# A four-sublayer decoder step on eight cores: x tiles loaded ahead of the weights, one ring for all PSUM banks, the next tile's norm ahead of the second group's products, and the program's last block in halves

## The reference

```python
h = x + 0.5 * rmsnorm(swiglu(rmsnorm(x, ffn1_pre_g), gate1, up1, down1), ffn1_post_g)   # FFN 1, 2816 wide
n = rmsnorm(h, mix_pre_g)
b_a, c_a, h_a, u, v = split(n @ w_in)                   # five parts of 512 columns
y_a = b_a * causal_dwconv(conv_prev, c_a * h_a, conv_w) # depthwise, 3 taps
v_n = rmsnorm(v per head of 64, v_norm_g)
y_b = u * (tril(w_s) @ v_n + b_s)                       # per head, over chunks of 128 tokens
h = h + rmsnorm(concat(rmsnorm(y_a, out_g_a), rmsnorm(y_b, out_g_b)) @ w_out, mix_post_g)
h = h + 0.5 * rmsnorm(swiglu(rmsnorm(h, ffn2_pre_g), gate2, up2, down2), ffn2_post_g)
h = h + rmsnorm(sigmoid(h @ ple_w_gate) * (p_emb @ ple_w_proj), ple_post_g)
```

## Time and profile before

| | us |
|---|---|
| median of 3 runs | 1360.84 |
| the profiled execution, whole time | 1360.08 |
| its span on the slowest core (core 2) | 1359.0 |
| shortest span of a core | 1348.5 |
| TensorE busy in that span | 1300.9 |
| VectorE busy | 523.6 |
| ScalarE busy | 410.3 |

### The profile page before, as it was taken

How to read it: one execution, slowest core, us unless ns; L and a number is a source line. 1 busy time by engine, 2 the same in 40 slices (tenths; PEclk the granted TensorE clock), 3 DMA queues, 4 the chain that set the end, 5 groups by cost and what they waited for, 6 DMA issues and landing times.

```text
span 1359.0 us, 18605 instructions; the slowest of 8 cores (1348.5 to 1359.0 us)
## 1 busy us (share of the span) xinstructions
PE 1300.9 (96%) x6770; PEld 650.7 (48%) x6770; DVE 523.6 (39%) x691; ACT 410.3 (30%) x858; POOL 94.3 (7%) x185
## 2 busy tenths in 40 slices
PE   6999999999989999999998999999999799999995
PEld 5566654455535666644433344444444344444442
DVE  3322223357776222213356322124467822212337
ACT  3311112344455111111165211123434611111136
POOL 1100000001001100000001000000010010000000
PEclk8999999999989999999989899999999899999998
DMA  9998322129715963231299983421396297433223
GB/s 214 180 211 181 63 47 47 28 57 164 129 26 103 169 108 63 48 69 26 53 201 232 224 160 67 75 43 31 68 166 116 57 158 143 78 56 62 32 39 124
DMA packets 88185, 139.87 MB, mean 103 GB/s; under 512 B 58272, under 2 KB 58528, under 8 KB 87456
## 3 DMA queue, kind: packets, MB, share of 16 engines
q0 software_dynamic: 25296, 90.25, 40.2%
q1 hardware_dynamic: 62800, 48.43, 13.6%
HBM read 206.03 MB, written 9.51 MB: 159 GB/s over the span
## 4 chain that ended last, share of the span: by engine, by line
PE 84%; DVE 6%; DMA 4%; issue 3%; ACT 2%; DVEq 0%; SPq 0%; ACTq 0%
PE ps L218 55%; PE ps L553 24%; PE ps L542 3%; DVE nT L227 2%; DVE zsc L227 2%; DMA h<-xT 1%; DVE big L231 1%; DMA y<-big 1%; DVE big L227 1%; DMA big<-xT 1%; ACT sg L223 1%; PE ps L498 1%; DVE nbr L227 1%; ACT big L223 1%; ACT L223 0%
## 5 line engine op out<-in xcount | busy, mean ns | idle before, releaser
L218 PE MATMUL ps<-nT,ring 128*128 128x384 bf16 (+1 forms) x4160 | 779.5, 349 | 18.8 <-DVE zsc L227 9.1
L218 PEld LDWEIGHTS ps<-nT,ring 128*128 128x128 bf16 x4160 | 407.9, 98 | 386.3 <-issue 35.4
L231 DVE TENSOR_TENSOR big<-ps,sg 128x384 bf16<-128x384 f32 (+1 forms) x220 | 134.1, 611 | 495.2 <-PE ps L218 476.0
L553 PE MATMUL ps<-ring,big 128*128 128x512 bf16 x1320 | 285.5, 379 | 4.4 <-DVE big L231 4.4
L223 ACT ACTIVATE sg<-ps 128x384 f32<-128x384 f32 (+1 forms) x237 | 126.8, 536 | 508.9 <-PE ps L218 499.9
L553 PEld LDWEIGHTS ps<-ring,big 128*128 128x128 bf16 x1320 | 128.9, 98 | 160.8 <-issue 6.0
L259 POOL DMA_DIRECT2D ring<-w x170 | 89.9, 537 | 1088.4 <-PE ps L218 499.6
L223 ACT ACTIVATE big<-ps 128x1024 bf16<-128x1024 f32 (+4 forms) x88 | 75.3, 870 | 222.6 <-PE ps L553 189.9
L227 DVE SCALAR_TENSOR_TENSOR zsc<-ps,st,gains 128x1024 f32<-128x1024 f32 x51 | 65.4, 1282 | 192.0 <-ACT st L223 191.7
L553 PE MATMUL ps<-ring,nT 128*128 128x512 bf16 x480 | 108.3, 386 | 5.7 <-DVE big L231 5.7
L553 PEld LDWEIGHTS ps<-ring,nT 128*128 128x128 bf16 x480 | 47.4, 99 | 65.6 <-issue 12.0
(11 more groups left out here) (65 smaller groups left out, 365.2 us busy)
## 6 DMA issues: line engine op xcount, KB each, us to landing
ring<-w POOLq DMA_DIRECT2D x170, 512.0 KB, 14.3
h<-x SPq DMA_DIRECT2D x17, 512.0 KB, 28.0
y<-big SPq DMA_DIRECT2D x13, 512.0 KB, 3.4
gains<-gain SPq DMA_DIRECT2D x12, 512.0 KB, 10.0
h<-xT SPq DMA_DIRECT2D x3, 1536.0 KB, 16.6
big<-xT SPq DMA_DIRECT2D x2, 2048.0 KB, 14.7
y<-zsc SPq DMA_DIRECT2D x4, 512.0 KB, 2.9
big<-pT POOLq DMA_DIRECT2D x2, 512.0 KB, 8.0
```

The source lines that it names most:

```text
L218: ins = nc.tensor.matmul(out_ap, l, r, start=(i == 0), stop=(i == n - 1))
L231: return DVE.mark(nc.vector.tensor_tensor(out=out, in0=in0, in1=in1, op=op))
L553: ins = nc.tensor.matmul(o.t, lhs(k), sv, start=(k == 0), stop=(k == nk - 1))
```

## The change

Five edits, all of order and buffers; the products computed are the same.

- **PSUM and waits.** One counter for all eight banks: `get_bank` takes the next, `get_pair` the next whole pair, skipping a bank where the count is odd. A block of a down projection waits for the products of its own tile (`hm[tile]`) and not for the last product of all. `post_apply` is turned round: VectorE first multiplies the banks by the gain, which waits for the square alone and frees the pair, then one scalar_tensor_tensor adds `zsc` * rstd to `h`.
- **Start.** Tile 0 of x comes in four DMAs and tile 1 in two, and the squares wait for their parts. POOL issues fill 0 only when the first half of tile 1 has landed. Tile 2 waits for fill 0. `warm_up` gets 70 matmuls behind the first statistic and 16 behind the second (40 behind the second before).
- **`ple` of pass 0.** The squares of tile (1, 0) stand behind the sigmoids of group 0, the statistic in group 1 behind the gate of block 3, with its result in a free gain buffer in place of a bank, and the application ahead of group 1's products.
- **End.** The last group of two blocks goes through `last_two`: the gate of block 7 in two halves of 512 columns, the gain applied before the rstd is known, and block 7 stored in halves.

```diff
-    def get_tp():
-        b = banks[6 + rot["tp"] % 2]
-        rot["tp"] += 1
-    def get_pair(n=3):
-        i = rot["pair"] % n
-        rot["pair"] += 1
+    def get_bank():
+        i = rot["n"] % 8
+        rot["n"] += 1
+        return take(banks[i])
+
+    def get_pair():
+        i = (rot["n"] + 1) // 2 % 4
+        rot["n"] = 2 * i + 2
+        return ps[i], take(banks[2 * i]), take(banks[2 * i + 1])
...
-    xt_load(PASSES[0], 0)
+    xt_load(PASSES[0], 0, 4)
     ev_gc = gc_sem.add(nc.sync.dma_start(out=gc_t[:], in_=gcol_d))
-    xt_load(PASSES[0], 1)
+    xt_load(PASSES[0], 1, 2)
...
-    for _ in range(2):
-        issue_next()
     ev_pc = pchain(nc.gpsimd.memset(carry_t[:], 0.0))
-    xt_load(PASSES[0], 2, [ev_pc])
+    POOL.wait(xt_ev[0, 1][0])
+    issue_next()
+    xt_load(PASSES[0], 2, 1, fill_ev[0][1])
...
-        r, e3 = st
-        DVE.wait(h_ev[b])
-        e = stt([e3, gain_ev[gi], zfree[zi]], zsc_t[:, zi, :], pt[:], r, gain(gi))
+        r, e3, e1 = st
+        e = tt([e1, gain_ev[gi], zfree[zi]], zsc_t[:, zi, :], pt[:], gain(gi), ALU.mult)
         lo.free = hi.free = e
-        h_ev[b] = zfree[zi] = tt([e], h_t[:, b, :], h_t[:, b, :], zsc_t[:, zi, :], ALU.add)
+        h_ev[b] = zfree[zi] = stt([e, e3, h_ev[b]], h_t[:, b, :], zsc_t[:, zi, :], r, h_t[:, b, :], ALU.mult, ALU.add)
...
+            for b in grp:
+                pair = gate(b, lastg and b == grp[-1])
+                if N is not None and b == 3:
+                    xs["st"] = x_stat(N, 0, xs["sq"], gain(base + NGAIN + GMPRE)[:, 0:512])
+                    xt_load(N, 1, 1, [xstat_ev[1, 0]])
+                sigmoid(b, pair)
+            if N is not None and gi == 0:
+                xs["sq"] = x_square(N, 0, [guards["zsc"]])
+            if N is not None and gi == 1:
+                gain_load(base + NGAIN + GMPRE, [x_apply(N, 0, *xs["st"], [gate_ev[3]])])
...
+            for i, (cols, ev) in enumerate(half):
+                es = act([ev, gb_guard(b1)], out=gb(b1)[:, cols], in_=pt[:, cols], func=AF.Sigmoid)
+                ez = tt([es, e1[1]], gb(b1)[:, cols], pe[:, cols], gb(b1)[:, cols], ALU.mult)
+                z1.append(tt([ez], zg[1][:, cols], gb(b1)[:, cols], gp[:, cols], ALU.mult))
+                if i == 0:
+                    sq.append(act([ez], out=junk[:, cols], in_=gb(b1)[:, cols], func=AF.Square, accum_out=q[:, 0:1]))
+                    sq.append(act([sq[0]], out=q[:, 0:1], in_=q[:, 0:1], func=AF.Copy, bias=EPS, scale=1.0 / D))
+                else:
+                    r, e3, _ = rstd_rest(r0)
+                    sq.append(act([ez], out=junk[:, cols], in_=gb(b1)[:, cols], func=AF.Square, accum_out=q[:, 1:2]))
...
     first = x_stat(PASSES[0], 0, x_square(PASSES[0], 0))
+    warm_up(70)
     x_apply(PASSES[0], 0, *first)
     second = x_stat(PASSES[0], 1, x_square(PASSES[0], 1))
-    warm_up(40)
+    warm_up(16)
```

More of the change, by code:

```diff
@@ L105, in __init__, with tile_of @@
         self.nb = len(rows)
+    def tile_of(self, b):
+        return [ti for ti in range(len(self.tiles)) if b in self.blocks(ti)][0]
     def blocks(self, ti):
@@ L183, in build_program, with take @@
     banks = [Bank(ps[i // 2][:, 512 * (i % 2):512 * (i % 2) + 512]) for i in range(8)]
[L184 to L188, removed]
+    rot = {"n": 0}
+    def take(b):
         assert b.free is not None
@@ L355, in build_program, with xt_load @@
     xt_ev = {}
-    def xt_load(P, ti, wait=None):
+    def xt_load(P, ti, parts=1, wait=None):
         c0, w = P.tiles[ti]
@@ L862, in embed, with store, gate, sigmoid @@
             return pair, ev
+        def store(b, z, cols=slice(0, D)):
+            SP.wait(z)
+            return y_sem[b].add(nc.sync.dma_start(out=y_d[P.rows[b]:P.rows[b] + 128, cols], in_=gb(b)[:, cols]))
+        def gate(b, last):
+            pair, gate_ev[b] = proj_block(P, b, 8, lambda k: nT_t[:, k, b * 128:(b + 1) * 128], 4, fg, [nT_ev[b]], last)
+            del nT_ev[b]
+            return pair
+        def sigmoid(b, pair):
+            pt, lo, hi = pair
+            sig[b] = act([gate_ev[b], gb_guard(b)], out=gb(b), in_=pt[:], func=AF.Sigmoid)
+            lo.free = hi.free = sig[b]
@@ new lines, in product, with finish @@
+        def product(b, pair, ev):
+            pt, lo, hi = pair
+            zev[b] = tt([ev, sig[b]], gb(b), pt[:], gb(b), ALU.mult)
+            lo.free = hi.free = zev[b]
+        def finish(b, st):
+            r, e3 = st[0], st[1]
+            e = stt([e3, gain_ev[base + GPLE]], gb(b), gb(b), r, gain(base + GPLE))
+            nxt["stt"] = e
+            e = tt([e], gb(b), gb(b), h_t[:, b, :], ALU.add)
+            out_ev[b] = store(b, e)
+            if N is not None and b < N.nb:
+                h_free[b] = e
@@ L864, in ple @@
+        sig, zev = {}, {}
         for gi, grp in enumerate(groups):
             lastg = gi == len(groups) - 1
[L866 to L881 removed]
@@ L893, in ple @@
-            if N is not None and gi == 0:
-                xs["st"] = x_stat(N, 0, xs["sq"], get_tp)
-            for b in grp:
-                r, e3 = st[b]
-                e = stt([e3, gain_ev[base + GPLE]], gb(b), gb(b), r, gain(base + GPLE))
-                nxt["stt"] = e
-                e = tt([e], gb(b), gb(b), h_t[:, b, :], ALU.add)
-                SP.wait(e)
-                out_ev[b] = y_sem[b].add(nc.sync.dma_start(out=y_d[P.rows[b]:P.rows[b] + 128, :], in_=gb(b)))
-                if N is not None and b < N.nb:
-                    h_free[b] = e
+            if N is None and lastg:
+                last_two(*grp)
+                break
```

149 lines of the change are left out of this document (82 added, 67 removed).

## The result

| | before | after |
|---|---|---|
| median of the runs, us | 1360.26 | 1334.17 |
| profiled execution, span of the slowest core | 1359.0 | 1331.8 |
| span of the fastest core | 1348.5 | 1326.5 |
| mean span of the eight cores | 1352.9 | 1330.0 |

The account below looks back on a forecast made before the run. TensorE, busy 1300.9 of 1359.0 us, was taken as the bound, movable only by its idle stretches and lower-clock matmuls. Terms 5.5 + 4.3 + 6.4 + 9 + 5.5 + 0 = 30.7, from 1360.1 to 1329.4 us; range 1321 to 1340.

Parts of the forecast that it names:

- start: Kernel start: x tiles 0 and 1 come alone, weight work begins at 19, second slice at 22.7; gain 5.5 us.
- four entries: Entries of the four down projections: waits for the very last hidden product go; gain 4.3 us.
- mixer, pass 0: Way out of pass 0's mixer: block 0 takes free banks, output projection's block 1 starts near 382.8; gain 6.4 us.
- mixer, pass 1: Way out of pass 1's mixer: FFN 2 starts 7.1 us earlier, at the upper clock level; gain 9 us.
- ple, pass 0: ple of pass 0: no wait for xT, application fills VectorE's idle time, stores leave 5.4 us earlier; gain 5.5 us.
- end: Kernel end: last group in halves, VectorE's end at 1356.9 against 1356.3 before, smaller last store; gain 0.
- half of tile 1 at 12 ... Fill 0 is issued at 12: Start: half of tile 1 lands at 12 us, fill 0 is issued then, its halves land at 19 and 22.7.
- the stores hold pass 1: Rival, chance 0.2: DMA bounds 676 to 752, stores land at their old time, ple gives 0; 1335 us.
- A tail of about 13 to 14 us: Sign at the end: time left behind the last matmul, about 13 to 14 us.
- The fills come too late: Rival, chance 0.1: DMA left empty, first units starve; start gives 0 if split tiles pay latency in turn; 1335 us.
- A clock that gives less to a denser TensorE: Rival "slower", chance 0.02: denser TensorE work is granted less clock, a further 61 us at the lower level eats the gain.
- a gain of over 2%: Whole kernel: time below the border of 1333.6 us, chance 0.70; within 2% had 0.28.

Follow-up runs that it names:

- e12_whole_tiles: e9_combined with x tiles 0 and 1 in one transfer each, fill 0 issued when tile 0 has landed: 1319.95 us, ratio 0.9719.
- e6_early_fill: The changed kernel with fill 0 issued behind the last part of tile 0, not the first half of tile 1: lowest time 1330.55 us.
- e9_combined: The changed kernel with pass 1's first hidden slices exchanged in the buffer, fill 0 issued behind tile 0's last part, and the old end: 1317.82 us, ratio 0.9712.
- e3_ring_ple: The kernel before with ple's new order and one ring for all banks, everything else as before: 1341.36 us, ratio 0.9883.
- e1_start: The kernel before with the start's edits alone: 1353.97 us, ratio 0.9976.
- e8_old_end: The changed kernel with the old end (block 7's gate whole, whole stores): 1333.88 us.

## Why the prediction came out as it did

Predicted and measured on core 2, whose rows the sum was made from (entry waits taken out of the others):

| term | predicted | bounds | measured |
|---|---|---|---|
| start | 5.5 | 3 to 6.5 | 2.3 |
| four entries | 4.3 | 3.5 to 4.4 | 4.4 |
| mixer, pass 0 | 6.4 | 5.4 to 6.6 | 5.95 |
| mixer, pass 1 | 9 | 7 to 9.4 | 9.4 |
| ple, pass 0 | 5.5 | 0 to 10 | 5.6 |
| end | 0 | -1 to 1 | -0.4 |
| sum | 30.7 | | 27.2 |

**Start: the term that failed.** The step was "half of tile 1 at 12 ... Fill 0 is issued at 12". The half landed at 13.4 on core 2, and POOL went on at 14.0 (between 13.1 and 14.2 on the eight cores). The step took tile 0's landing at 9.96 as that of a tile "with two fills competing". But the fills had taken nothing from it: whole and without a fill under way (e12_whole_tiles) it landed at 8.1 to 9.8 us, in the trace of before at 8.2 to 9.9. In four parts it was even later, 10.0 to 11.0 in the changed kernel. The time from issue to landing of the whole fill was nearly right: 22.7 - 12 = 10.7 us was assumed, 10.5 is the measured mean (13.6 to 24.2), 11.2 on core 2. The second slice of the first unit, which was to start at 22.7, started at 26.4 on core 2. Of these 3.7 us, 2.0 are the late issue and 0.5 the longer landing (the second half was there at 25.2 and not at 22.7). The last 1.2 are the clock: behind 3.71 us of standing the first slice ran at the lower level, and the first 112 matmuls took 20.04 us, where they had taken 18.36. The forecast had already taken off 0.3 from its 5.8, and 3.2 us are missing at D1. The bound of 3 allowed for the empty DMA, not for the clock behind it. Two of the signs that the prediction named were missed with it: the first matmul on weights came at 19.1 to 22.1 us, not near 19 to 20, and the wait for fill 0's second half was 0.8 to 1.5 us on five cores, not at most 1. e6_early_fill and e9_combined show the step mended: with the issue at 11 the start gives 5.4 us against before by D1 less its entry wait (203.4 - 197.0 - 1.0).

**Entries**: right in place and size. The first matmul of each down projection follows within 0.05 us.

**Mixer of pass 0**: right. Block 1 started at 379.16; against D1 that is 5.5 us earlier than before. ScalarE was late next, as said, by 1.82 us, and the whole came to 0.45 us less than the sum had.

**Mixer of pass 1**: right, at the upper bound. FFN 2 started 7.0 us earlier against D3 (7.1 was said) and at the upper level, and nothing was lost at the second tile. e3_ring_ple shows the mechanism: with the ring alone the wait for a bank is gone.

**ple: the size right by luck, the reason half right.** The prediction credited the application, which fills VectorE's idle time, with the earlier stores. On core 2 the last add of group 2 ended 60.8 us behind the first gate before, and 55.5 after. But in e1_start, with the old order, half of the cores have 55.5 too: those on which the tile of x was in time. So the stores' 5.3 us on core 2 were the late tile (the 3.38 us and the matmuls at the lower level behind them) alone, and other cores had lost less of them: 2.5 us in the mean. What filling the idle time won, together with the ring, is the first unit, 49.6 to 43.4 us, and that went into the wait for the stores. The rival "the stores hold pass 1" was therefore true of most cores: D2 to D3 became 2.0 us shorter in the mean, 1.2 of them by the entry, so that the term was some 0.9 there. It was 5.6 on core 2 because that core had lost most to the late tile in the one execution that was profiled. e1_start shows how little of this is the new order's: with the old one, core 2 had 294.2 us from D2 to D3, against 300.4 before and 293.6 after. That the sum came within 3.5 us of the profiled execution, and the time inside the forecast's own range, is in part luck. That the fastest core's span shrank by 22 us and the slowest one's by 27 is the same effect.

**End**: inside its bounds, on the wrong side. e8_old_end prices it at 0.5 us. "A tail of about 13 to 14 us" was wrong (14.7), since TensorE is done earlier with the ring and the chain behind it is VectorE's.

**The other rivals.** "The fills come too late" was true in its first half, the empty DMA, which with the clock behind it cost 3 us rather than all of the start; its second half, that split tiles pay one after another, fell with e12_whole_tiles (some 1.3 us in place of 8). A clock that gives less to a denser TensorE didn't show: the mean granted clock rose from 0.980 to 0.989 on core 2, and to 0.994 and more in e9_combined, the densest of all.

The forecast was 4.8 us too low. 3.5 of it is the sum against the profiled execution (1332.9): 3.2 the start, 0.4 the end, as much the mixer of pass 0, less what the other terms gave beyond their sizes. The rest, 1.2 us, is the median above that execution. The chances leaned too far to a gain of over 2% (0.70); what came had 0.28.

## What to carry to other kernels

An edit that moves work forward is worth only what the next guard lets through. Here 6 us won in ple became 1, until the buffer that the next stage writes first was one that nobody was still reading; ask of each stage start which buffer it overwrites, and who reads it last. A wait on TensorE is to be costed with the matmuls at the lower level behind it, which came to some 4 us beside 7 of waiting in one place. And where a transfer is held back to give another one the DMA, issue it so early that it is there when the queue runs dry, not when the other has landed: here the queue ran dry near 14 us, the issue at 10.8 gave 2.3 us against 13.6, and the issue at 7.8 took them back. A sum made on the slowest core is right for the time only if what made it the slowest is one of the terms; look at a second core as well.

## What the hardware showed that was not expected

- The clock stays down for longer than the wait. On core 2 of the changed kernel, behind the waits between 725 and 739 us, the 10 us from 740 on had a mean granted clock of 0.70 at 94% busy, and 0.95 and 0.84 in the two windows ahead of them.
- Fills issued by POOL at the very start of the program did not slow the first tile of x: as a whole tile it landed at 8.2 to 9.9 us with them queued (before) and at 8.1 to 9.8 without (e12_whole_tiles). Tile 1 did feel them, 16.9 to 18.7 against 14.2 to 16.9.
- Six x transfers of 384 and 768 KB in place of two cost little: the end of tile 0 came 1.3 us later and that of tile 1 0.4, by the means of e9_combined and e12_whole_tiles.
- One tile of x that is late under fills cost one core 0.6 us and another 5.3 in the same run (last add 56.1 to 60.8 us behind the first gate, 55.5 where it is in time), the largest part of the spread between the cores.
